# One decoder layer on one core: the passage from output projection to feed-forward rearranged

## What is computed

```
m = mix @ w_out                                  # output projection
x = x + gt1 * rmsnorm(m, g_post_mix)
h = rmsnorm(x, g_pre_ffn) * (1 + sc2) + sh2
f = (silu(h @ w_ffn_gate) * (h @ w_ffn_up)) @ w_ffn_down
x = x + gt2 * rmsnorm(f, g_post_ffn)
```

## Time and profile before

| what | us |
|---|---|
| median of 3 runs | 1550.08 (1549.39 to 1553.08) |
| the profiled execution, its own time | 1549.46 |
| its span, first to last instruction | 1547.9 |
| PE busy | 1453.0 (94%) |
| DVE busy | 932.2 (60%) |
| ACT busy | 665.2 (43%) |

### The profile page before, as it was taken

How to read it: one execution, slowest core, us unless ns; L and a number is a source line. 1 busy time by engine, 2 the same in 40 slices (tenths; PEclk the granted TensorE clock), 3 DMA queues, 4 the chain that set the end, 5 groups by cost and what they waited for, 6 DMA issues and landing times.

```text
span 1547.9 us, 28791 instructions
## 1 busy us (share of the span) xinstructions
PE 1453.0 (94%) x11304; PEld 1286.7 (83%) x11304; DVE 932.2 (60%) x1021; ACT 665.2 (43%) x1277; POOL 96.0 (6%) x188
## 2 busy tenths in 40 slices
PE   6769999998889999998799999999999999999996
PEld 2237787887668777786699999999999999999996
DVE  2143499996777656446566665666665664445445
ACT  1023377666655544234544344343444343334333
POOL 0000311112322200100000000000000000000000
PEclk9879999999999999999999999999999999999999
DMA  9989999989999967995666656656656555555551
GB/s 370 420 311 357 381 352 392 346 328 386 383 374 325 340 240 254 389 341 213 230 178 177 188 176 178 182 178 182 177 176 187 178 172 185 183 178 178 180 171 56
DMA packets 138272, 394.43 MB, mean 255 GB/s; under 512 B 12875, under 2 KB 17138, under 8 KB 125378
## 3 DMA queue, kind: packets, MB, share of 16 engines
q1 hardware_dynamic: 117730, 319.39, 60.6%
q0 software_dynamic: 20464, 74.00, 12.4%
HBM read 382.14 MB, written 11.21 MB: 254 GB/s over the span
## 4 chain that ended last, share of the span: by engine, by line
PE 73%; DVE 11%; DMA 10%; issue 3%; ACT 2%; POOLq 0%; SPq 0%; POOL 0%; ACTq 0%; DVEq 0%
PE ps L1772 21%; PE ps L1773 21%; PE ps L1774 21%; DMA ada_s<-in_w_ada 4%; PE ps L1698 3%; DVE k_page L1196 3%; DMA k_page<-in_cache_k 3%; DVE w_lo L1152 2%; PE ps L1904 1%; DMA ada_r<-in_w_ada 1%; PE ps L1730 1%; DMA v_page<-in_cache_v 1%; DMA raw<-in_w_in 1%; DMA k_page<-in_cache_v 1%; ACT w_hi L664 1%
## 5 line engine op out<-in xcount | busy, mean ns | idle before, releaser
L1772 PE MATMUL ps<-h_hi,w_hi 128*128 128x264 f32 x2304 | 669.1, 290 | 16.0 <-DVE h_lo L1118 7.8
L1773 PE MATMUL ps<-h_lo,w_hi 128*128 128x264 f32 x2304 | 659.4, 286 | 0.0
L1774 PE MATMUL ps<-h_hi,w_lo 128*128 128x264 f32 x2304 | 658.9, 286 | 0.0
L1772 PEld LDWEIGHTS ps<-h_hi,w_hi 128*128 128x128 f32 x2304 | 439.4, 191 | 62.2 <-issue 42.0
L1629 DVE TENSOR_TENSOR w_lo<-raw,w_hi 128x1024 fp32r<-128x1024 f32 x260 | 314.4, 1214 | 291.5 <-ACT w_hi L979 290.1
L979 ACT ACTIVATE w_hi<-raw 128x1024 fp32r<-128x1024 f32 x264 | 278.0, 1059 | 403.4 <-PE ps L1774 397.6
L1773 PEld LDWEIGHTS ps<-h_lo,w_hi 128*128 128x128 f32 x2304 | 438.6, 190 | 0.1
L1774 PEld LDWEIGHTS ps<-h_hi,w_lo 128*128 128x128 f32 x2304 | 437.2, 190 | 0.0
L1152 DVE TENSOR_TENSOR w_lo<-raw,w_hi 128x1024 fp32r<-128x1024 f32 x132 | 160.9, 1221 | 157.0 <-ACT w_hi L664 156.8
L664 ACT ACTIVATE w_hi<-raw 128x1024 fp32r<-128x1024 f32 x128 | 134.5, 1054 | 198.9 <-PE ps L1774 174.7
L1773 PE MATMUL ps<-act_lo,w_hi 128*128 (+1 forms) x704 | 200.4, 285 | 0.0
(11 more groups left out here) (308 smaller groups left out, 1152.7 us busy)
## 6 DMA issues: line engine op xcount, KB each, us to landing
ada_r<-in_w_ada SPq DMA_DIRECT2D x64, 1024.0 KB, 8.7
raw<-in_w_in SPq DMA_DIRECT2D x96, 512.0 KB, 7.7
raw<-in_w_ffn_gate SPq DMA_DIRECT2D x88, 512.0 KB, 3.7
raw<-in_w_ffn_up SPq DMA_DIRECT2D x88, 512.0 KB, 3.8
raw<-in_w_ffn_down SPq DMA_DIRECT2D x88, 512.0 KB, 4.4
ada_s<-in_w_ada SPq DMA_DIRECT2D x32, 1024.0 KB, 13.8
k_page<-in_cache_k POOLq DMA_DIRECT2D x64, 512.0 KB, 7.5
v_page<-in_cache_v POOLq DMA_DIRECT2D x38, 512.0 KB, 7.5
```

Of the source, the lines that this page charges most:

```text
L1772: mm(out, w_hi, xh, start=first, stop=False)
L1773: mm(out, w_hi, xl, start=False, stop=False)
L1774: return mm(out, w_lo, xh, start=False, stop=last)
```

## The change

- **Last two units tile by tile.** `last_units` takes units 126 and 127 together, 12 matmuls per output tile, so that the four tiles are done one after another. ACT squares each bank straight from PSUM and copies it with the gate scale in the same instruction; DVE adds three squares to the folded ones and gates the samples' columns; PE multiplies by ones twice, not five times. ACT makes `w_hi` of only two feed-forward units ahead of this, two behind the root; DVE makes two `w_lo` ahead.
- **Roots in fewer steps.** Four of the seven (`rs_sum`, roots 1, 5, 6, 7): ACT takes Ln straight from PSUM with scale and eps as bias, while DVE makes `rvar` once Ln is done. In all seven the correction has three operations.
- **Smaller pieces.** x in five pieces of 4, 4, 4, 2 and 2 chunks; the samples' scaling once for all; `x_scale` of the last two quarters is done in the next stage. h in eight pairs of chunks: `h_hi` is written directly with the shift (one operation less), `h_lo` by one fused operation per chunk.
- **Last conditioning part out of the slots.** Steps 48 to 52 stand behind the first sum, 53 and 54 behind the first two pieces' sums, 55 to 59 behind the sums of x; 60 to 63 stay. Loads 53 and 54 leave slots 122 and 123 for SP's queue behind unit 3.
- Besides: semaphores joined (`x_kept` and `x_back`, `masks` and `vgs_zero`), one more memset on POOL at the start (`eps_t`), and counts renumbered.

The diff, cut to its core:

```diff
@@ -253,10 +254,9 @@
-A_SLOT.update({48: 117, 49: 119, 50: 121})
...
-A_LOAD.update({32: 94, 33: 95, 34: 98, 38: 101, 39: 102, 48: 113, 49: 116, 50: 118, 51: 120, 52: 121, 53: 122, 54: 123})
+A_LOAD.update({32: 94, 33: 95, 34: 98, 38: 101, 39: 102, 48: 113, 49: 116, 50: 118, 51: 120, 52: 121})
@@ -278,6 +278,8 @@
+PIECES = ((0, 4), (4, 8), (8, 12), (12, 14), (14, 16))
@@ -455,7 +458,7 @@
-    for n in range(55, 60):
+    for n in range(53, 60):
@@ -643,9 +647,16 @@
-        s.activation(dst, dst, ACT.Exp, scale=-0.5).then_inc(rs_ready, 1)
-    rs(rstd[:, :], rvar[:, :], 1)
+        s.activation(dst, dst, ACT.Exp, scale=-0.5).then_inc(rs_ready, 2)
+    def rs_sum(bank, n, nsum):
+        act.wait_ge(sums_done, nsum)
+        s.activation(rstd[:, :], ps[:, bank, 0:T], ACT.Ln, scale=1.0 / D, bias=eps_t[:, 0:1]).then_inc(rs_ready, 1)
+        act.wait_ge(rs_ready, 2 * n - 1)
+        s.activation(rstd[:, :], rstd[:, :], ACT.Exp, scale=-0.5).then_inc(rs_ready, 1)
+    rs_sum(6, 1, 1)
@@ -969,33 +980,44 @@
-            for m in range(3):
+            for m in range(3 if st // UPC < NIN + NOUT - 1 else 0):
...
-    evac(NSLOT // UPC - 1, 3)
...
-    for u in range(4):
+    for u in range(2):
...
-    rs(rstd[:, :], rvar[:, :], 5)
+    for m in range(MT):
+        if m < 3:
+            act.wait_ge(bank_done, 3 * (NIN + NOUT - 1) + m + 1)
+        else:
+            act.wait_ge(unit_used, W_FFN)
+        s.activation(SQD[:, KC - MT + m, :], ps[:, m, 0:T], ACT.Square).then_inc(last_sq, 1)
+        act.wait_ge(scl_ready, 1)
+        s.activation(MT_[:, KC - MT + m, 0:TP], ps[:, m, 0:TP], ACT.Copy,
+                     scale=scale_t[:, KC - MT + m, 0:1]).then_inc(bank_out, 1)
+    rs_sum(6, 5, 2)
+    for u in range(2, 4):
+        hi_n(W_FFN, u)
...
-        act.wait_ge(scl_ready, 1)
+        act.wait_ge(scl_ready, 2)
...
-    for q in range(4):
-        act.wait_ge(x_new, q + 1)
-        s.activation(SQD[:, 4 * q:4 * q + 4, :], X[:, 4 * q:4 * q + 4, :], ACT.Square).then_inc(sq_ready, 1)
-        if q < 3:
-            x_scale(q)
-    rs(rstd[:, :], rvar[:, :], 6)
-    x_scale(3)
+    for i, (k0, k1) in enumerate(PIECES):
+        act.wait_ge(x_new, i + 1)
+        s.activation(SQD[:, k0:k1, :], X[:, k0:k1, :], ACT.Square).then_inc(sq_ready, 1)
+        if i < 2:
+            x_scale(i)
+    rs_sum(7, 6, 3)
@@ -1018,14 +1040,19 @@
-    for q in range(4):
-        act.wait_ge(h32_ready, 4 + q + 1)
-        for k in range(4 * q, 4 * q + 4):
-            ins = s.activation(F_LO[:, k, 0:TP], F_LO[:, k, 0:TP], ACT.Identity, bias=MOD[:, 3 * KC + k, 0:1])
-        link(ins)
-        s.activation(H_HI[:, 4 * q:4 * q + 4, :], F_LO[:, 4 * q:4 * q + 4, :], ACT.Copy).then_inc(hhi_ready, 1)
-    for u in range(4, UPC + 1):
-        hi_n(W_FFN, u)
+    for p in range(UPC):
+        act.wait_ge(h32_ready, 4 + p + 1)
+        for k in (2 * p, 2 * p + 1):
+            ins = s.activation(H_HI[:, k, 0:TP], F_LO[:, k, 0:TP], ACT.Identity, bias=MOD[:, 3 * KC + k, 0:1])
+        if p == 0:
+            act.wait_ge(hs_ready, 1)
+            ins = s.activation(H_HI[:, :, TP:T], F_LO[:, :, TP:T], ACT.Copy)
+        ins.then_inc(hhi_ready, 1)
+        if p in (1, 2):
+            x_scale(p + 1)
+        if 3 <= p:
+            hi_n(W_FFN, p + 1)
@@ -1095,13 +1122,15 @@
-    def rstd_of(dst, var, src, width, n):
+    def rstd_of(dst, var, src, width, n, behind=False):
+        if behind:
+            dve.wait_ge(rs_ready, 2 * n - 1)
...
-        dve.wait_ge(rs_ready, n)
+        dve.wait_ge(var_ready, n)
+        dve.wait_ge(rs_ready, 2 * n)
...
-        link(v.tensor_tensor(var, var, dst, ALU.mult))
-        link(v.tensor_scalar(var, var, -0.5, 1.5, ALU.mult, ALU.add))
-        link(v.tensor_tensor(dst, dst, var, ALU.mult))
+        link(v.scalar_tensor_tensor(var, var, -0.5, dst, ALU.mult, ALU.mult))
+        link(v.scalar_tensor_tensor(dst, var, 1.5, dst, ALU.add, ALU.mult))
@@ -1580,38 +1610,66 @@
+    for u in range(2):
+        lo(W_FFN + u)
+    for m in range(MT - 1):
+        dve.wait_ge(last_sq, m + 1)
+        ins = v.tensor_tensor(SQD[:, 0, :], SQD[:, 0, :], SQD[:, KC - MT + m, :], ALU.add)
+        if m < MT - 2:
+            link(ins)
+    ins.then_inc(sq_ready, 1)
...
-    v.tensor_tensor(SQD[:, KC - MT:KC, :], MT_[:, KC - MT:KC, :], MT_[:, KC - MT:KC, :], ALU.mult).then_inc(sq_ready, 1)
-    dve.wait_ge(sq_ready, 6)
-    link(gated(MT_, KC - MT, KC))
+    link(v.tensor_tensor(MT_[:, KC - MT:KC, TP:T], ps[:, 0:MT, TP:T], scale_t[:, KC - MT:KC, 1:NC], ALU.mult))
...
-    v.scalar_tensor_tensor(scale_t[:, :, :], MOD[:, 4 * KC:5 * KC, :], 1.0, gain.unsqueeze(2).to_broadcast([P, KC, NC]),
-                           ALU.add, ALU.mult).then_inc(scl_ready, 1)
+    v.scalar_tensor_tensor(scale_t[:, :, :], MOD[:, 4 * KC:5 * KC, :], 1.0,
+                           gain.unsqueeze(2).to_broadcast([P, KC, NC]), ALU.add, ALU.mult).then_inc(scl_ready, 1)
...
-    rstd_of(rstd[:, :], rvar[:, :], ps[:, 6, 0:T], D, 5)
-    dve.wait_ge(x_back, 16)
-    dve.wait_ge(scl_ready, 1)
-    for q in range(4):
-        cs = slice(4 * q, 4 * q + 4)
-        add_quarter(MT_, XOLD, q, 0)
-        link(v.tensor_tensor(F_LO[:, cs, TP:T], X[:, cs, TP:T], scale_t[:, cs, 1:NC], ALU.mult))
-    lo(W_FFN)
-    lo(W_FFN + 1)
+    rstd_of(rstd[:, :], rvar[:, :], ps[:, 6, 0:T], D, 5, behind=True)
+    dve.wait_ge(x_moved, 32)
+    for i, (k0, k1) in enumerate(PIECES):
+        cs = slice(k0, k1)
+        link(v.tensor_tensor(MT_[:, cs, :], MT_[:, cs, :], rstd[:, :].unsqueeze(1).to_broadcast([P, k1 - k0, T]),
+                             ALU.mult))
+        v.tensor_tensor(X[:, cs, :], MT_[:, cs, :], XOLD[:, cs, :], ALU.add).then_inc(x_new, 1)
+    dve.wait_ge(x_new, len(PIECES))
+    dve.wait_ge(scl_ready, 2)
+    link(v.tensor_tensor(F_LO[:, :, TP:T], X[:, :, TP:T], scale_t[:, :, 1:NC], ALU.mult))
+    for u in range(2, 4):
+        lo(W_FFN + u)
...
-    rstd_of(rstd[:, :], rvar[:, :], ps[:, 7, 0:T], D, 6)
-    for q in range(4):
-        cs = slice(4 * q, 4 * q + 4)
-        dve.wait_ge(x_scaled, q + 1)
-        link(v.tensor_tensor(F_LO[:, cs, :], F_LO[:, cs, :], rstd[:, :].unsqueeze(1).to_broadcast([P, 4, T]), ALU.mult))
-        v.tensor_tensor(F_LO[:, cs, TP:T], F_LO[:, cs, TP:T], MOD[:, 3 * KC + 4 * q:3 * KC + 4 * q + 4, 1:NC],
-                        ALU.add).then_inc(h32_ready, 1)
-        if q >= 1:
-            low_h(4, q - 1)
-        if q in (1, 2):
-            lo(W_FFN + 1 + q)
-    low_h(4, 3)
+    rstd_of(rstd[:, :], rvar[:, :], ps[:, 7, 0:T], D, 6, behind=True)
+    def pair_norm(p):
+        dve.wait_ge(x_scaled, p // 2 + 1)
+        cs = slice(2 * p, 2 * p + 2)
+        v.tensor_tensor(F_LO[:, cs, 0:TP], F_LO[:, cs, 0:TP], rstd[:, 0:TP].unsqueeze(1).to_broadcast([P, 2, TP]),
+                        ALU.mult).then_inc(h32_ready, 1)
+    def pair_low(p):
+        dve.wait_ge(hhi_ready, 4 + p + 1)
+        for k in (2 * p, 2 * p + 1):
+            ins = v.scalar_tensor_tensor(H_LO[:, k, 0:TP], F_LO[:, k, 0:TP], MOD[:, 3 * KC + k, 0:1],
+                                         H_HI[:, k, 0:TP].bitcast(F32), ALU.add, ALU.subtract)
+        if p == 0:
+            ins = v.tensor_tensor(H_LO[:, :, TP:T], F_LO[:, :, TP:T], H_HI[:, :, TP:T].bitcast(F32), ALU.subtract)
+        ins.then_inc(h_ready, 1)
+    pair_norm(0)
+    link(v.tensor_tensor(F_LO[:, :, TP:T], F_LO[:, :, TP:T], rstd[:, TP:T].unsqueeze(1).to_broadcast([P, KC, TS]),
+                         ALU.mult))
+    v.tensor_tensor(F_LO[:, :, TP:T], F_LO[:, :, TP:T], MOD[:, 3 * KC:4 * KC, 1:NC], ALU.add).then_inc(hs_ready, 1)
+    for p in range(1, UPC):
+        pair_norm(p)
+        if p == 1:
+            dve.wait_ge(hs_ready, 1)
+        pair_low(p - 1)
+        if p >= 4:
+            lo(W_FFN + p)
+    pair_low(UPC - 1)
@@ -1721,17 +1779,17 @@
-    def sums(src, bank, n0, done, step=None, after=None):
-        for q in range(4):
+    def sums(src, bank, n0, done, pieces, step=None, after=None):
+        for i, (k0, k1) in enumerate(pieces):
...
-                step(q)
-            pe.wait_ge(sq_ready, n0 + q + 1)
-            for k in range(4 * q, 4 * q + 4):
+                step(i)
+            pe.wait_ge(sq_ready, n0 + i + 1)
+            for k in range(k0, k1):
...
-            if q == 3:
+            if k1 == KC:
...
-                after(q)
+                after(i)
@@ -1989,8 +2047,26 @@
+    def last_units():
+        pe.wait_ge(lo_ready, W_FFN)
+        g = NIN + NOUT - 1
+        for m in range(MT):
+            for u in (W_FFN - 2, W_FFN - 1):
+                for kk in range(2):
+                    k = 2 * ((u + 4) % UPC) + kk
+                    cs = slice(kk * CG + m * P, kk * CG + (m + 1) * P)
+                    ins = products(ps[:, m, 0:T], HI[:, u % 4, cs], LO[:, u % 4, cs], H_HI[:, k, :], H_LO[:, k, :],
+                                   False, u == W_FFN - 1 and kk == 1)
+            if m < MT - 1:
+                ins.then_inc(bank_done, 1)
+        ins.then_inc(unit_used, 2)
...
```

(21 more changed lines are left out.)

50 lines of the change are left out of this document (27 added, 23 removed).

## The result

| what | before | after |
|---|---|---|
| median of the first set of runs | 1551.47 us (1549.39 to 1553.08, 4 runs) | 1535.14 us (1533.82 to 1538.81, 4 runs) |
| ratio, first set | | 0.9897, 95% interval 0.9884 to 0.9910 |
| second set, further below | 1551.09 (11 runs) | 1537.95 (1536.45 to 1538.55, 4 runs), 0.9911, 0.9895 to 0.9926 |
| the profiled execution, its own time / its span | 1549.46 / 1547.9 | 1533.82 / 1532.2 |
| PE busy | 1453.0 (94%) | 1456.9 (95%) |

The changed kernel is 1.0% faster: 15.7 us between the two profiled executions.

The account below looks back on a forecast made before the run. PE was taken to bound the feed-forward, behind a chain through DVE and ACT. Gains of 14.0 us up to unit 4, 0.7 last root and 0.3 roots in slots sum to 15.0, giving 1535.1 us; range 1532.5 to 1539.5.

Parts of the forecast that it names:

- Steps out of the slots: Projection slots: a conditioning step there costs 1.09 us; three leave, so the projection ends 3.27 us earlier, bounds 0 and 3.3.
- Last units: Projection's end to first sum: only tile 3 is left, sum ready 1.05 us behind instead of 4.3, 3.2 of chain.
- Root: Each root on the path: 2.4 us instead of 3.11, saving 0.7 at each of three, the last root included.
- x and its sums: First root to last sum of x: sums end at 727.7, PE and not x bounds, full clock after 1 us gap.
- h: Second root to feed-forward: rstd at 730.1, `h_lo` of pair 0 at 733.3, while PE does steps 55 to 59.
- SP's queue: Conditioning loads 53 to 59: one step lands every 2.5 us, step 59 at 732.6, so the feed-forward starts at 733.75.
- Clock in the first units: First four feed-forward units with their steps: 16.5 us at full clock, where before they took 17.8.
- Loads come late: Rival, chance 0.20: load 53 takes 9.7 us, those after stand 4.9 behind, feed-forward starts 4.8 later: 1539.9 us.
- The clock falls anyway: Rival, chance 0.15: low clock for the first products of x (1.35) and first feed-forward unit (1.3): 1537.8 us.
- Slots bound by weights: Rival, chance 0.08: the steps' 3.3 us return as waits for `raw`, projection ends at 713.9: 1538.4 us.
- nothing reaches the end: Rival, chance 0.02: the feed-forward catches up on DMA or otherwise, so the time is 1549 us.
- slower: Rival, chance 0.03: PE stays at the lower clock through the whole stage, 20 us against 15 gained: 1555 us.

Follow-up runs that it names:

- old roots: The changed kernel with all seven roots as before (`rvar`, Ln, Exp, four DVE operations, one behind the other): 1539.05 us, ratio 0.9927.

## Why the prediction was right, and where not

Forecast 1535.1, range 1532.5 to 1539.5. The first median is 1535.14, the second 1537.95, and all eight runs of the change (1533.82 to 1538.81) lie inside. The mechanism was right: a chain shortened, PE's gaps filled and the slow clock avoided. That the first median agrees to 0.04 us is luck. The medians of the first set differ by 16.3 us and those of the second by 13.1, where 15.0 was forecast. Step by step:

- **Steps out of the slots**: 3.27 expected, 3.60 measured (1.2 each). Mis-sized by 0.1 a step: the working stopped at the first matmul behind the step (681.98 in the trace before), but the second comes 0.23 behind that one and not 0.12.
- **Not bound by weights**: right; PE was busy without a break from the transposes to the projection's end, and P was 35.4 in every kernel with the steps out, 39.0 in every one with them in.
- **Last units**: the sum 1.05 us behind the end expected; the product pair ended 709.85, 1.2 behind 708.67. Saved on the chain 3.1, where I had 3.2.
- **Root**: 2.4 expected, 2.46 measured at both; 0.67 saved at the end, for 0.7. Ln with its pointer operand took 0.48, Exp 0.42. The Trainium skill (ScalarE: Activation LUTs, "What ACT_TABLE_LOAD costs") puts such an operand at 93 ns. The difference here is 60 ns, between Ln, which also reads PSUM, and Exp, which reads SBUF; no run has the operand as the only difference.
- **x and its sums**: from the first sum to the last sum of x I had 16.05, and it took 16.0 (709.85 to 725.85). Five steps take 4.5 us in a row instead of 5.0, and that only lengthened the wait behind them, 1.79 instead of 1: the squares of the first quarter set the start of the products (6.2 behind the sum, 6.05 expected), so at this point x is the bound and not PE, as I wrote. The clock held, as I took it; with 2.49 us (old roots) it did not, so this rested on 0.7 us. The fifth piece, which I costed without asking what it bought, is worth nothing.
- **h**: 3.2 from rstd to the first `h_lo`; 728.34 to 731.37 is 3.03.
- **SP's queue**: the term with the largest error in its size. Step 59 was to land 19.8 us behind the issue of load 53 (4.8, and six more at 2.5). The issue was at 710.91, by the row of SP below, and step 59 started upon its landing at 731.81: 20.9, so 1.1 later, and in the second trace 0.7 later still (712.17 to 733.80). I wrote that h and DMA would both be late next; in fact the loads alone were, by 1.4 us.
- **Clock in the first units**: 16.5 expected, 16.47 in the first trace, 18.33 in the second.
- **The sum**: unit 4 was to come 75.65 behind the transposes and came at 76.29 and 79.74. The first trace is hence 0.64 worse by its own clock than forecast, and met the forecast because its transposes came 1.61 early where 0.3 was expected. Of that 1.61 no run shows how much the roots in slots 91 to 100 gave, and the 0.3 is not shown either: the same stretch varies by up to 5.8 us between traces of kernels alike up to there.

```profile
710.91 11.56 SPq L380 DMA_DIRECT2D ada_r<-in_w_ada  x7
```

```profile
712.17 11.56 SPq L380 DMA_DIRECT2D ada_r<-in_w_ada  x7
```

(SP's own queue in the timelines of the first and the second trace of the change: it takes up the seven loads, 53 to 59, from 710.91 and 712.17 on.)

**The rivals.** *Loads come late* (0.20): the mechanism is there in both traces, at 1.1 and 1.8 us more than expected instead of the 4.9 that I priced. *The clock falls anyway* (0.15): its price of 2.7 was for the first products and the first unit; in the second trace it happened, at the last step and the first unit, for 2.7 (0.86 and 1.86), behind waits for loads of 1.4 and 1.5 us. What the prediction had wrong is that it held these two rivals apart: waits for late loads are gaps too, and in one of two executions the clock fell behind them (0.80 in 730 to 735 and 0.52 in 735 to 740, which is the sign that I had named for the second rival). *Slots bound by weights*, *nothing reaches the end* and *slower* found nothing: in the first trace the granted clock is 1.00 from the transposes to the end, and U to the end is 782.9 us (783.6 before, with the old last root).

## What to carry to other kernels

Where PE is bound behind a stage and idles inside it, count two things: the chain that ends the stage, and each gap of PE, since a gap can cost the clock of the work behind it (here every one of 2.1 us and more did, for 1.3 to 2.9 us). Work of another kind that is wanted later belongs in the longest gap, with its loads issued so early that none is waited for, and taking it out of there can cost more than it weighs. To judge changes of 1 or 2 us in a kernel whose runs differ by 5, count positions from a mark just ahead of the change, and take more than one trace of it: two traces of this change differ by 3.45 us at unit 4.

## What was not expected of the hardware

- The gaps of PE that went with a lower clock, in these traces. Ahead of the four products of x the clock held at 1.78 or 1.79 us in six traces and fell at 2.49, 3.50, 4.16 and 4.36. Ahead of the first feed-forward matmul it held at 1.15 us in five traces and at 1.80 in one, and fell at 2.11, 2.86, 5.26 and 7.83. Between steps, waits of 0.71 and 1.48 us with one step between them held, 1.41 and 1.49 fell. So the last gap alone does not decide it. The Trainium skill (TensorE: Matmul & The Clock Gate, "HAM oscillation — how this bites in real kernels") tells of a kernel whose bursts of matmuls start cold each time behind a wait for DMA. Its waits are longer than the ones here; the second trace, with 1.41 and 1.49 us, did the same, the first, with 0.71 and 1.48, did not.
- Eight useless products made the kernel with steps in the slots 2.40 us faster to unit 4.
- Loads in one queue, issued alike (load 53 is issued 37.92 us behind the transposes in both traces of the change), landed 0.7 us apart between two executions.
